# A hybrid encoder step: output projection in three single-pass products, row maxima as columns, single first loads of k and q

## What is computed

```python
def fox_block(qi, cq, qpos, k, v, ck):
    logits = jnp.einsum('bqhd,bkhd->bhqk', qi, k) * scale
    logits = logits + cq[..., :, None] - ck[..., None, :]
    logits = jnp.where(mask, logits, -jnp.inf)
    p = jax.nn.softmax(logits, axis=-1)
    return jnp.einsum('bhqk,bkhd->bqhd', p, v)

mix = jnp.concatenate([o_fox, o_gdn], axis=-1)
h = x + jnp.einsum('bte,ed->btd', mix, w_o)
hn = rmsnorm(h, norm_ffn_w)
up = jnp.einsum('btd,df->btf', hn, w_up)
```

## Time and profile before

| | |
|---|---|
| median of 3 runs | 4025.61 us (4022.91 to 4026.85) |
| profiled execution, its own time | 4023.51 us |
| its span, first to last instruction | 4021.8 us |
| PE busy | 3810.0 us (95%) |
| DVE, ACT, POOL busy | 1624.0, 1212.8, 313.8 us |
| mean granted clock of TensorE | 0.977 of 2.4 GHz |
| `project`, `heads` | 0 to 732.7 us, 732.7 to 2104.8 us |
| `mix` | 2104.8 to 2401.5 us |
| `ffn_up`, `ffn_down` | 2401.5 to 3486 us, 3486 us to the end |

### The profile page before, as it was taken

One profiled execution on the slowest core, in us unless ns is written; L12 is line 12 of the kernel. 1 busy time (PEld: TensorE's weight loads), 2 busy tenths in 40 slices (PEclk: granted clock), 3 DMA queues, 4 the chain that ended last, 5 costly groups with the idle time before them and its releaser, 6 DMA issues. The chain is left out here.

```text
span 4021.8 us, 54872 instructions
## 1 busy us (share of the span) xinstructions
PE 3810.0 (95%) x20813; PEld 3210.6 (80%) x20813; DVE 1624.0 (40%) x3357; ACT 1212.8 (30%) x2223; POOL 313.8 (8%) x352
## 2 busy tenths in 40 slices
PE   7999999699999999999989988999999999899998
PEld 7999999577777777776754448999999999688886
DVE  4000477545444455444422334444444444432222
ACT  4112222233333333332212333333333333231111
POOL 3000000212111111112100000000000000000000
PEclk9999999799999999999989999999999999899999
DMA  4221221510222202134323221111111111252222
GB/s 146 69 68 62 60 74 65 92 39 23 59 44 44 52 23 46 31 107 145 132 75 116 94 83 50 45 43 56 45 43 45 45 43 46 92 163 78 80 80 66
DMA packets 322301, 278.65 MB, mean 69 GB/s; under 512 B 121666, under 2 KB 283826, under 8 KB 322055
## 3 DMA queue, kind: packets, MB, share of 16 engines
q1 hardware_dynamic: 301871, 247.21, 20.7%
q0 software_dynamic: 5040, 18.09, 1.3%
q10 hardware_dynamic: 15228, 11.10, 1.0%
HBM read 190.70 MB, written 85.65 MB: 69 GB/s over the span
## 5 line engine op out<-in xcount | busy, mean ns | idle before, releaser
L2337 PE MATMUL bank<-hn_hi,up_w_parts 128*128 128x436 f32 (+1 forms) x3520 | 981.8, 360 | 10.3 <-DVE up_w_parts L2412 10.3
L2337 PEld LDWEIGHTS bank<-hn_hi,up_w_parts 128*128 128x128 f32 x3520 | 662.3, 188 | 42.1 <-issue 10.5
L2337 PE MATMUL bank<-hn_lo,up_w_parts 128*128 128x436 f32 (+1 forms) x1760 | 633.0, 360 | 0.0
L2337 PEld LDWEIGHTS bank<-hn_lo,up_w_parts 128*128 128x128 f32 x1760 | 331.5, 188 | 19.1
L332 PE MATMUL bank<-proj_wh,proj_xh 128*128 128x256 f32 (+1 forms) x1088 | 310.1, 285 | 0.0
L332 PE MATMUL bank<-proj_wl,proj_xh 128*128 128x256 f32 (+1 forms) x1088 | 307.2, 282 | 0.0
L332 PE MATMUL bank<-proj_wh,proj_xl 128*128 128x256 f32 (+1 forms) x1088 | 307.1, 282 | 0.0
L2383 ACT COPY up_raw<-bank 128x436 f32<-128x436 f32 (+1 forms) x220 | 110.3, 502 | 642.3 <-PE bank L2337 612.3
L1432 PE MATMUL bank<-heads_p_pT,heads_p_v 128*65 128x512 f32 (+3 forms) x640 | 287.4, 531 | 10.2 <-issue 10.1
L2408 DVE TENSOR_SCALAR up_hist<-up_raw 128x2 f32 (+2 forms) x264 | 45.0, 170 | 550.4 <-ACT up_acc L2387 546.1
L2069 PE MATMUL bank<-mix_w,mix_mT 128*128 128x512 f32 x544 | 240.5, 600 | 10.7 <-DMA mix_w<-in_w_o_dram 8.3
(11 more groups left out here) (403 smaller groups left out, 6637.2 us busy)
## 6 DMA issues: line engine op xcount, KB each, us to landing
up_w<-in_w_up_dram SPq DMA_DIRECT2D x44, 512.0 KB, 4.8
down_g_raw<-scratch_g SPq DMA_DIRECT2D x110, 192.0 KB, 2.3
scratch_g<-up_acc SPq DMA_DIRECT2D x88, 218.0 KB, 2.0
heads_s_k<-in_cache_fox_k_dram SPq DMA_DIRECT2D x8, 2048.0 KB, 12.6
heads_s_v<-in_cache_fox_v_dram SPq DMA_DIRECT2D x8, 2048.0 KB, 8.1
heads_d_qkvT<-scratch_gch SPq DMA_DIRECT2D x17, 768.0 KB
down_y<-in_w_down_dram SPq DMA_DIRECT2D x22, 512.0 KB, 3.6
scratch_gch<-proj_work SPq DMA_DIRECT2D x48, 218.0 KB, 1.9
```

Source lines behind the costliest of these rows:

```text
L2337: mm = pe.matmul(bank[:, pair(n) + e, 0:width], w_parts[:, a, part, e, k, :], x[:, k, cols], start=(k == 0 and m == 0), stop=(k == KD - 1 ...
```

## The change

**In `mix`** the products are three single-pass ones (`three`, L2110). `w_o` is loaded during `heads` into the two buffers `k` of `Sample`, once the last streams' keys are turned (`load_wo`, L1644), and split in `mix` slice by slice (`w_part` on ACT, `w_rest` on DVE). Both halves of the mixers' tile are rounded by ACT (`copy_in`) and their remainders taken by DVE (`rest_in`), into the places in `hn_hi` and `hn_lo` that the tile's result will fill later. h lives in the place of `hn_lo`, as pieces of 512 bytes, and is normalised in place, after its store. The norm's factor is formed by POOL with a power instead of by ACT. The norm's weights are applied by ACT and DVE as they split, in eight operations of 128 columns each. The loop is written out, and the outgoing transposes of tile t-1 stand inside the products of tile t.

**In `Prompt`** DVE splits the column of maxima into its rounded part and remainder, two dependent operations more, as columns 96 and 97 of `top_parts`, which is 98 columns wide and otherwise zero. The product with the negated identity, now fp32r, gives both rows at once, ACT copies them to `q_hi`, and DVE only counts up `row_free`.

**At the start of `heads`** keys and queries of head 0 are loaded once, POOL copies them to the other half of the columns, and the load of the values moves from ACT's queue to SP's.

```diff
--- before.py
+++ after.py
-        self.sel = ph.sb("p_sel", [self.KM, 1])
-        self.top_lo = ph.sb("p_top_lo", [self.KM, BANK], F32R)
+        self.top_parts = ph.sb("p_top_parts", [P, 2, 4, self.KM], F32R)
...
-            for e in range(2):
+            for e in range(2 if h else 1):
...
         yield -30.0
         load_k(0)
+        yield -19.0
+        load_v(0)
...
-        for e in range(2):
-            act.dma_start(self.qtok[:, :, e * FD:(e + 1) * FD],
-                          io["q_tok"][0:SEQ, 0:FD].rearrange("(n p) d -> p n d", p=P)).then_inc(s["q_loaded"], 16)
-        act.dma_start(self.v[:, 0, :, 0:FD], io["v_p"][:, 0:FD].rearrange("(n p) d -> p n d", p=P)) \
-            .then_inc(s["v_loaded0"], 16)
+        act.dma_start(self.qtok[:, :, 0:FD], io["q_tok"][0:SEQ, 0:FD].rearrange("(n p) d -> p n d", p=P)) \
+            .then_inc(s["q_loaded"], 16)
...
         step = Step(pool, s["edges_ready"])
         step(nc.gpsimd.memset(self.v[:, :, :, FD], 1.0))
-        step(nc.gpsimd.memset(self.k_lo[96:98].bitcast(F32), 1.0))
+        step(nc.gpsimd.memset(self.top_parts[:].bitcast(F32), 0.0))
         for a in range(2):
             step(nc.gpsimd.memset(self.k_lo[FD:96, a].bitcast(F32), 0.0))
             step(nc.gpsimd.memset(self.q_hi[FD:96, a].bitcast(F32), 1.0))
+            if a == 0:
+                for tile, loaded in ((self.ktok, s["k_loaded"]), (self.qtok, s["q_loaded"])):
+                    pool.wait_ge(loaded, 16)
+                    nc.gpsimd.tensor_copy(tile[:, :, FD:], tile[:, :, 0:FD]).then_inc(loaded, 16)
+                    pool.wait_ge(loaded, 32)
+        step(nc.gpsimd.memset(self.k_lo[96:98].bitcast(F32), 1.0))
 
     def store(self, sp, G):
...
-                mm = pe.matmul(self.row_bank(r)[:, i * P:(i + 1) * P], spread(self.top[:, G % 2, i:i + 1], [P, P]),
+                mm = pe.matmul(self.row_bank(r)[0:self.KM, i * P:(i + 1) * P], self.top_parts[:, G % 2, i, :],
                                self.r.minus[:], start=True, stop=True)
...
-                G = tag[1]
-                yield at + 1.6
+                h, g = divmod(tag[1], self.NG)
+                yield at + 1.0
                 act.wait_ge(s["row_mm"], r + 1)
-                if G >= 1:
-                    act.wait_ge(s["row_free"], self.use["m", G - 1] + 1)
-                else:
-                    act.wait_ge(s["sel_ready"], 1)
-                nc.scalar.activation(self.top_lo[96:98], bank[96:98], ACT.Copy, scale=self.sel[96:98]) \
-                    .then_inc(s["m_ready"], 1)
+                nc.scalar.copy(self.q_hi[96:98, h % 2, g * BANK:(g + 1) * BANK], bank[96:98]).then_inc(s["m_ready"], 1)
             elif tag == ("c", 0):
...
-                nc.vector.tensor_reduce(self.top[:, G % 2, :], self.low[:, G % 2, :, 0:g + 1], AX.X, ALU.max) \
-                    .then_inc(s["top_ready"], 1)
+                top, hi, lo = self.top[:, G % 2, :], self.top_parts[:, G % 2, :, 96], self.top_parts[:, G % 2, :, 97]
+                nc.vector.tensor_reduce(top, self.low[:, G % 2, :, 0:g + 1], AX.X, ALU.max).then_inc(s["top_step"], 1)
+                if G == 0:
+                    dve.wait_ge(s["edges_ready"], 7)
+                dve.wait_ge(s["top_step"], 2 * G + 1)
+                nc.vector.tensor_copy(hi, top).then_inc(s["top_step"], 1)
+                dve.wait_ge(s["top_step"], 2 * G + 2)
+                tt(lo, top, hi.bitcast(F32), ALU.subtract).then_inc(s["top_ready"], 1)
 
         def maxima(r, G):
-            h, g = divmod(G, self.NG)
             dve.wait_ge(s["m_ready"], G + 1)
-            tt(self.q_hi[96:98, h % 2, g * BANK:(g + 1) * BANK], self.row_bank(r)[96:98],
-               self.top_lo[96:98].bitcast(F32), ALU.subtract).then_inc(s["row_free"], 1)
+            dve.wait_ge(s["row_free"], r)
+            dve.sem_inc(s["row_free"], 1)
...
+        def load_wo(n):
+
+            sp.wait_ge(s["kt_mm"], self.NK * (DB - 1 + n))
+            place = self.k[(DB - 2 + n) % 2][:].rearrange("p n f -> p (n f)").rearrange("p (k d) -> p k d", d=self.c["D"])
+            src = io["w_o"][0].rearrange("(k p) d -> p k d", p=P)
+            half = src.shape[1] // 2
+            sp.dma_start(place, src[:, n * half:(n + 1) * half, :]).then_inc(s["wo_loaded"], 16)
...
+            if b >= DB - 3 and b + 1 < DB:
+                yield self.at(b) + 35.0
+                load_wo(b - (DB - 3))
...
             def load_m(t):
-                sp.dma_start(m_tok[:], io["mix_tok"][rows(t), :]).then_inc(m_loaded, 16)
+                if t >= 1:
+                    sp.wait_ge(s["in_mm"], 2 * t)
+                sp.dma_start(own[:], io["mix_tok"][rows(t), :]).then_inc(s["m_loaded"], 16)
 
             def load_x(t):
-                sp.dma_start(x[:], io["x_s"] if t is None else io["x_p"][rows(t), :]).then_inc(x_loaded, 16)
+                if t >= 1:
+                    sp.wait_ge(s["h_ready"], ND * t)
+                if t == LATE:
+                    sp.wait_ge(s["in_mm"], 2 * NT)
+                src = io["x_s"] if t == NT - 1 else io["x_p"][rows(t), :]
+                sp.dma_start(x_place(t), src.rearrange("t (k c) -> t k c", c=P)).then_inc(s["x_loaded"], 16)
+
+            def store_h(t):
+                sp.wait_ge(s["h_ready"], ND * t + ND)
+                sp.dma_start(io["h_tok"][rows(t), :].rearrange("t (k c) -> t k c", c=P), h(t)).then_inc(s["h_stored"], 16)
 
             load_m(0)
-            sp.dma_start(norm_rows[:], io["norm_ffn_w"].rearrange("l (k p) -> (l k) p", p=P)).then_inc(small_loaded, 16)
-            sp.dma_start(w[:], io["w_o"][0].rearrange("(k p) n -> p k n", p=P)).then_inc(w_loaded, 16)
...
+            def three(t, n, k):
+                m_hi, m_lo = turned(t)
+                for m, (a, b) in enumerate(((m_hi, w_hi), (m_hi, w_lo), (m_lo, w_hi))):
+                    mm = pe.matmul(prod_bank(t, n), a[:, k, :], b[:, k, n * BANK:(n + 1) * BANK],
+                                   start=(k == 0 and m == 0), stop=(k == KM - 1 and m == 2))
+                return mm
+
+            def first_products():
+                pe.wait_ge(s["in_lo"], 2)
+                for k in range(KM):
+                    if k == HB:
+                        turn_in(1)
+                    pe.wait_ge(s["w_split"], k + 1)
+                    for n in range(ND):
+                        mm = three(0, n, k)
+                        if k == KM - 1:
+                            mm.then_inc(s["prod_mm"], 1)
 
...
             def products(t):
-                pe.wait_ge(in_out_a, t + 2)
-                pe.wait_ge(in_out_v, t + 2)
-
-                pe.wait_ge(h_ready, 2 * t + 2)
+                pe.wait_ge(s["in_lo"], 2 * t + 2)
+                if t >= 2:
+                    pe.wait_ge(s["h_ready"], ND * (t - 1))
                 for n in range(ND):
                     for k in range(KM):
-                        mm = pe.matmul(bank[:, 2 + n, :], mT[:, k, :], w[:, k, n * BANK:(n + 1) * BANK],
-                                       start=(k == 0), stop=(k == KM - 1))
-                    mm.then_inc(prod_mm, 1)
+                        if n == 1 and k == HB:
+                            turn_out(t - 1)
+                        mm = three(t, n, k)
+                    mm.then_inc(s["prod_mm"], 1)
 
             def turn_out(t):
-                pe.wait_ge(hn_ready, t + 1)
+                pe.wait_ge(s["hn_ready"], t + 1)
                 for n in range(2):
-
-                    pe.wait_ge(hT_ready, 2 * t + (n + 1))
+                    if t >= 1:
+                        pe.wait_ge(s["split_done"], 2 * (t - 1) + n + 1)
                     for k in range(HB):
-                        mm = pe.transpose(bank[:, 4 + n, k * P:(k + 1) * P],
-                                          hn[:, (n * HB + k) * P:(n * HB + k + 1) * P], c["ident"][:])
-                    mm.then_inc(out_mm, 1)
...
+            for t in range(1, NT):
+                if t + 1 < NT:
+                    turn_in(t + 1)
                 products(t)
...
+            def w_part(k):
+                nc.scalar.copy(w_hi[:, k, :], raw_w(k)).then_inc(s["w_hi_ready"], 1)
...
             def split_hi(t):
-                act.wait_ge(hT_ready, 2 * t + 4)
-                nc.scalar.copy(hn_hi[:, :, rows(t)], hT[:]).then_inc(hi_ready, 1)
-
-            act.sem_inc(in_out_a, 1)
+                for n in range(2):
+                    act.wait_ge(s["out_mm"], 2 * t + n + 1)
+                    if t == 0 and n == 0:
+                        act.wait_ge(s["small_ready"], 1)
+                    for k in range(n * HB, (n + 1) * HB):
+                        ins = nc.scalar.activation(hn_hi[:, k, rows(t)], in_bank(6 + n)[:, k % HB, :], ACT.Copy,
+                                                   scale=norm_w[:, k:k + 1])
...
+            w_part(0)
+            w_part(1)
...
+            def w_rest(k):
+                dve.wait_ge(s["w_hi_ready"], k + 1)
```

(34 more changed lines are left out.)

244 lines of the change are left out of this document (126 added, 118 removed).

## The result

| | before | changed |
|---|---|---|
| median of 4 runs each | 4025.49 us | 3957.32 us (3955.28 to 3959.77) |
| ratio, 95% interval | | 0.9834, 0.9821 to 0.9847 |
| span of the profiled execution | 4021.8 us | 3958.1 us |
| PE, DVE, ACT, POOL busy | 3810.0, 1624.0, 1212.8, 313.8 us | 3749.1, 1625.0, 1195.4, 332.6 us |
| mean granted clock | 0.977 | 0.976 |

Faster by 68.2 us; the prediction was 3956. The sum came out, though not every term. The profiled execution of the changed kernel was the slowest of its four (3959.77 us), so the spans of the two profiles differ by 63.7 us only.

What follows compares the result with a forecast made beforehand. TensorE (PE) was taken to bound the heads and output projection. Gains of 57.9 (projection), 9 (row maxima) and 3 (start) make 70 us off the profiled 4023.5, 3953.5; against the 4025.6 median that is 3956 us, range 3940 to 3984.

Steps and rivals of the forecast that it cites:

- The projection: Output projection: products, first tile and the stretch behind the last product together gain 57.9 us.
- The products: Projection tiles: three single-pass products at 0.226 us replace one fp32 product of 0.865; gain 46.8 us.
- The first tile: Start of the projection: `w_o` already loaded, 22.9 us instead of 33.0 until the second tile's products; gain 10.1 us.
- The end: Behind the projection's last product: about 10.5 us against 11.5, gain 1 us, between -2 and +3.
- The new wait: Projection: the in-place normalise waits for h's store; its landing L, taken as 4.5 us, stays hidden up to 5.75.
- The rival with a late store: Projection: a store or load lands a little late, L at 7, 20 us less gained, 3976 us; chance 10%.
- Start: Start of the heads: single loads and POOL copies bring keys 6.5 us sooner; gain 3 us, ends -4 and 8.
- the 760 that was named as the sign of being wrong: Start of the heads: POOL coming to the delta rule later than 760 us would show the prediction wrong.
- PE's order behind it: Start of the heads: delta-rule chain starts no sooner, but PE behind it, clear of key and query transposes, gains; 3 us.
- Row maxima: Heads, 32 groups: single-pass products save 12.2, longer waits cost 5.6, an earlier bank gives 2.4; gain 9 us.
- 14 x 0.4 = 5.6 us: Row maxima: PE, waiting for DVE in 14 of 32 groups, waits 0.4 us longer in each; costs 5.6 us.
- the heads give nothing: Rival: small DVE steps hold PE in every group and POOL comes late to the delta rule; 3968 to 3973, 8%.

Runs made afterwards that it cites:

- plain products: The changed kernel with one fp32 product per projection step in place of the three single-pass ones, remainders left out of the sum: 4003.43 us.
- the earlier transposes: The changed kernel with the projection's outgoing transposes two steps (6 products, 1.36 us) earlier within each tile: 3968.67 us.
- the fills first: The changed kernel with POOL's constant fills ahead of its waits for keys and queries at the start of the heads, run twice: 3950.70 and 3949.31 us.
- eight profiles with the conversion: Profiles whose row maxima are the changed kernel's chain of reduce, convert, subtract; first to last maxima 941.7 to 942.3 us without lost clock.
- two with the old maxima: Profiles of the kernel before and of the new projection with the old heads; first to last maxima 952.9 and 953.1 us without lost clock.
- the first pair: The first profiles of the kernel before and of the changed kernel; first to last maxima 956.3 and 950.2 us.
- the new projection: The kernel before with only the new projection, loads of `w_o` included, and the old heads: 3961.91 us.

## Why the prediction was right, and where it was not

**The projection, 57.9 us predicted, 61.1 measured.** The products: 27 in a row, 2203.05 to 2209.18, take 0.227 us each, as forecast, and a tile's 48 take 11.1 us from start to start, transposes left out, for 10.85. The Trainium skill's 215.7 ns ("TensorE: Matmul & The Clock Gate", "Wait — 56ns, not 53.3ns?"), which would have made the gain 8 us larger, is not met. The run with plain products gives the 47.6 back. The first tile: 22.9 predicted, 22.9 measured, products 7.4 us into the stage for 7.5. The end 10.4 for 10.5, in part by luck: the normalise starts 5.1 us behind the last product and not 6.5, and what follows the transposes takes 2.5 us and not 1.3. The 3 us too little are two things. One is the step "because the transposes stay the same": between single-pass products two sets cost 1.6 us and not 2.0, and a period is 12.70 instead of 12.85, 2 us in 14 periods. The other is a set too many: tile 15 has no incoming transposes behind it, since there is no tile 17, and takes 11.9 us where the sum has 12.85. Together the middle part is 201.45 instead of 204.6.

**The new wait.** "I take 4.5, hidden": the store landed in 5.3 us, limit 5.75. Hidden as forecast, but by 0.4 us and not by 1.25, as the earlier transposes showed. The rival with a late store was nearer than its 10% looked. Its mechanism is the right one; the size of L did not reach it.

**Start, +3 us predicted, about -2 measured.** This step failed. The sentence "POOL now has two copies, a larger memset, and the wait for the queries ahead of the memsets of the other half, 1.80 us each" does not name the fill of the rows of ones, 3.51 us, which had moved behind that wait as well. From queries at 748 the terms that it does name bring POOL to L1020 at some 755.4, and that fill makes it 759, so the forecast of 758 to 760 has room for it; what took POOL to 761.5, past the 760 that was named as the sign of being wrong, is that the queries came at 750.9 and not at 748. What failed is the next sentence: that with POOL no sooner than before PE would still gain from "PE's order behind it". With POOL's unit late, DVE's in-order queue held the low parts of the keys and PE with them, 7.54 us, so there was nothing to gain. The copy itself was cheaper than taken, 1.04 us for 1.6. The Trainium skill's port rule was weighed for the wrong place: the copies collided with nothing in the changed kernel (DVE's 0.76 and 2.25 stand there undisturbed), and the order of POOL's queue alone took the gain. With the fills first the start is 42.2 and 41.6, 3 us and more under the 45.2 before: the 3 us were there.

**Row maxima, 9 us predicted, 7.8 measured** as the mean of eight profiles with the conversion, 947.8, against 955.6 of two with the old maxima (945.4 to 950.6, and 954.8 and 956.3); 6.1 in the first pair. That these lie so near is luck. The term "14 x 0.4 = 5.6 us" rests on a misreading: the earlier trace rows counts PE and PEld together, PE itself waited in 7 groups, 7.1 us, so the term is 2.8, and it measured 1.8 (8.9 us in 9). The products gave more than their 12.2: with the lost clock off, PE's busy time in the middle fell by 16.7 us in the first pair, its idle time rose by 5.4, of which 1.8 ahead of the maxima, and the middle is 11.2 us shorter; over all profiles it is 942.0 against 953.0, 11.0 us. Why PE's busy time fell by more than the four products save is open, and the 2.4 us for the bank that comes free sooner can't be told apart in it. What the step did not have is the clock, which lost 5.8 us on average in the eight middles and 2.6 in the two old ones, and so took 3.2 us back. It also makes the rest 1.4 us longer in the first pair: 24.0 us lost against 22.5.

**The sum** of 70 us was nearly met (68.2 and 70.3) because +3 of the projection stand against -5 of the start and -1 to -3 of the maxima; these leave 65 to 67, and the rest is within what two profiles and medians of a few runs scatter. That the terms' errors are of both signs is luck. Of the rival "the heads give nothing" only the start came: the heads gave about 6 to 7 us beside the new projection (3961.91 to 3955.16).

## What to carry to other kernels

When work is moved behind a wait on an in-order queue, list everything that now stands behind that wait, fills too, and put what needs no data ahead of it: here that one order was worth some 6 us of start (47.9 to 42.2 and 41.6) and 4.5 to 5.5 us of the time. A store that is waited for in place is free only while its landing, not its issue, fits beneath the other work; see by how much, since the next tightening meets it. On the vector side, a small operation is not small beside POOL, and when one form is replaced, look whether the next operation meets POOL instead, as the subtraction did here. Take the lost clock off before two lengths are compared: here it turned a scatter of 5 us into one of 0.6. And ask of a view which engines it adds up.

## What was not expected of the hardware

- A conversion of 4 columns took 0.17 us in 28 groups and 0.32, 0.56, 0.71 and 1.15 in four, in the same places in seven profiles more; a reduction of the same size was never over 0.17, but the subtraction of two such columns behind it took up to 1.09.
- Two SBUF copies of 512 columns on DVE took 0.76 us alone and 1.91 and 2.45 beside POOL's copy and fills, which took 1.97 in place of 1.80 in one of the two runs.
- Over one stretch of the same 5380 PE instructions, busy time was 892.77 or 886.11 us as the clock was 0.99 or 1.00. Between profiles of the same code the clock took from 3.4 to 8.5 us of such a stretch, in which PE is busy 94% of the time. Many places of the dips repeat from run to run, not all. The gap of PE ahead of the maxima near 1050 is 1.57 us long before and after the change, and only the changed kernel shows a dip behind it, so that gap alone does not decide.
- POOL copied 128 x 1024 columns in 1.04 us, and filled 2 x 4096 in 3.51 and 32 x 2048 in 1.80: its price went by columns, not by partitions.
